# Finishing each token's row in its second expert unit instead of through a plane of partial rows (GLA and MoE block, fp32, one core)

## What is computed

```python
def second_block(...):
    ...
    h2 = rmsnorm_2(x, norm2_g[l])
    x = x + hier_moe(h2, ...)      # 4 groups x 8 experts, D_EXPERT = 256, two experts of one group per token
return rmsnorm_2(x, norm_f_g)

# one expert on its rows:
(jax.nn.silu(xb @ w_gate[e]) * (xb @ w_up[e])) @ w_down[e]
```

```
group 0:  44 50 40 25 15 34 20 12
group 1:  28 14 21 24 21 25 32 29
group 2:  89 43 53 51 35 47 40 14
group 3:   7 30 37 29 11 31 48 25
```

## Time and profile before

| | us |
|---|---|
| median of 3 runs (1300.69 to 1302.65) | 1300.85 |
| the profiled execution, its own time | 1302.32 |
| its span | 1300.0 |
| TensorE busy | 1267.6 (98%) |
| VectorE busy | 613.1 (47%) |
| ScalarE busy | 460.4 (35%) |
| GpSimd busy | 535.5 (41%) |

### The profile page before, as it was taken

The page is one execution under the profiler, slowest core; times in us unless marked ns, Lnnn a source line. Parts: engine busy times, 40 slices in busy tenths (PEclk is TensorE's granted clock), DMA queues, the critical chain, the costliest instruction groups (busy, mean ns, idle before and its releaser), DMA issues.

```text
span 1300.0 us, 18634 instructions
## 1 busy us (share of the span) xinstructions
PE 1267.6 (98%) x6670; PEld 968.7 (75%) x6670; DVE 613.1 (47%) x1162; ACT 460.4 (35%) x770; POOL 535.5 (41%) x685
## 2 busy tenths in 40 slices
PE   8999999999999999999999999999999999999986
PEld 6767777787888888888888788777888875555552
DVE  4868768725542422222225765757243265222225
ACT  5657534435434324133144534145322210000102
POOL 4633323334555655555545664424644211121100
PEclk9999999999999999999999999999999999999999
DMA  7422222112334433434333333312426989999995
GB/s 221 107 65 56 66 58 66 50 49 81 98 96 113 131 97 97 130 98 129 97 98 114 97 93 85 83 49 67 128 81 268 362 323 394 424 421 424 424 423 240
DMA packets 212157, 211.38 MB, mean 163 GB/s; under 512 B 31903, under 2 KB 193425, under 8 KB 200817
## 3 DMA queue, kind: packets, MB, share of 16 engines
q1 hardware_dynamic: 203104, 200.25, 45.8%
q0 software_dynamic: 5184, 8.29, 1.7%
q10 hardware_dynamic: 3796, 1.86, 0.5%
HBM read 205.76 MB, written 16.78 MB: 171 GB/s over the span
## 4 chain that ended last, share of the span: by engine, by line
issue 39%; POOL 31%; PE 26%; DMA 1%; DVE 1%; POOLq 0%; ACT 0%; SPq 0%; DVEq 0%; ACTq 0%
POOL wlo L661 31%; PE bank L2287 8%; PE bank L2304 4%; PE bank L1915 3%; PE bank L1917 3%; PE bank L1916 3%; PE side L1945 2%; DMA y<-y_rows 1%; PE bank L1956 1%; DMA y_rows<-xe,tabi 1%; PE side L1917 1%; PE side L1915 1%; PE side L1916 1%; PE side L2203 1%; PE bank L2419 0%
## 5 line engine op out<-in xcount | busy, mean ns | idle before, releaser
L661 POOL TENSOR_TENSOR wlo<-raw,whi 128x256 fp32r<-128x256 f32 x644 | 498.2, 805 | 524.4 <-ACT whi L785 524.2
L1916 PE MATMUL bank<-actB_lo,whi 128*128 128x512 f32 x608 | 236.7, 389 | 0.0
L1915 PE MATMUL bank<-actB_hi,whi 128*128 128x512 f32 x576 | 227.7, 395 | 0.5 <-POOL wlo L661 0.5
L1917 PE MATMUL bank<-actB_hi,wlo 128*128 128x512 f32 x576 | 224.4, 390 | 0.0
L785 ACT ACTIVATE whi<-raw 128x1024 fp32r<-128x1024 f32 x161 | 169.0, 1051 | 151.8 <-PE bank L1917 124.9
L1915 PE MATMUL bank<-actA_hi,whi 128*128 128x512 f32 x400 | 157.3, 393 | 0.6 <-DVE actA_lo L1201 0.6
L1916 PE MATMUL bank<-actA_lo,whi 128*128 128x512 f32 x400 | 156.1, 390 | 0.0
L1917 PE MATMUL bank<-actA_hi,wlo 128*128 128x512 f32 x400 | 156.1, 390 | 0.0
L2287 PE MATMUL bank<-gu,xeT 128*64 128x256 f32 x1088 | 127.7, 384 | 4.7 <-issue 2.2
L1916 PEld LDWEIGHTS bank<-actB_lo,whi 128*128 128x128 f32 x608 | 114.2, 188 | 24.1 <-issue 1.0
L1915 PEld LDWEIGHTS bank<-actB_hi,whi 128*128 128x128 f32 x576 | 108.1, 188 | 25.9 <-issue 2.3
(11 more groups left out here) (433 smaller groups left out, 1653.0 us busy)
## 6 DMA issues: line engine op xcount, KB each, us to landing
dn<-in_w_exp_down SPq DMA_DIRECT2D x32, 1024.0 KB, 16.0
raw<-in_w_in SPq DMA_DIRECT2D x57, 512.0 KB, 3.8
gu<-in_w_exp_gate SPq DMA_DIRECT2D x28, 1024.0 KB
gu<-in_w_exp_up SPq DMA_DIRECT2D x28, 1024.0 KB
raw<-in_w_up SPq DMA_DIRECT2D x32, 512.0 KB, 3.9
raw<-in_w_down SPq DMA_DIRECT2D x32, 512.0 KB, 3.6
raw<-in_w_out SPq DMA_DIRECT2D x16, 512.0 KB, 3.7
raw<-in_w_in SPq DMA_DIRECT2D x16, 256.0 KB, 3.1
```

Of the source, the lines that this page charges most:

```text
L661: ins = nc.gpsimd.tensor_tensor(wlo[:, slot, at], raw[:, slot, at], whi[:, slot, at].bitcast(F32), ALU.subtract)
L1915: mm(b[:, :], w_hi, hi[:, k, :], start=first, stop=False)
L1916: mm(b[:, :], w_hi, lo[:, k, :], start=False, stop=False)
L1917: ins = mm(b[:, :], w_lo, hi[:, k, :], start=False, stop=last)
```

## The change

The plane of 1,024 partial rows goes. In its place is part_rows, 512 rows of zeros. The unit that has a token first (in unit order) scatters its row there as before; the unit that has it second gathers that row into the token's place in its buffer (a row of it that is first is skipped), adds its own part, norms the whole row and stores it to the output by an indirect DMA. So that both units of a token are not next to each other, experts are now taken one from each group in turn: number n is expert n // 4 of group n % 4. `full` and `late` are worked out in that order. Unit 9's places are now 18 and 17, with number 16 in place 17; units 8 and 9 are "mixed", their tokens' other unit may be any. There are six row buffers instead of five; x is no longer halved. Rows are finished from unit 2 on.

Cut to its core, with the address changes, the overflow loops (not entered) and removed tail parts left out or shortened:

```diff
-GU_BUFS, D_BUFS, X_BUFS = 6, 8, 5
+GU_BUFS, D_BUFS, X_BUFS = 6, 8, 6
...
-    c = (n - 2 * EXTRA_AT + 1) // 2
-    return c - 1 if n % 2 else PAIRS - 1 if n == SPARE else c + PAIRS // 2 - 2
+    return 0 if n == SPARE - 1 else n - SPARE
...
-    return n if n < 2 * EXTRA_AT else None
+    return EPG * (n % NG) + n // NG if n < 2 * EXTRA_AT else None
...
+FINISH_FROM = 2
+MIXED_E = (EXTRA_AT, EXTRA_AT + 1)
...
-                for n in range(2 * q, 2 * q + 2):
-                    sp.dma_start(y2_rows[n * P:(n + 1) * P, :], zeros[:, :]).then_inc(S("y_zeroed"), 16)
+                sp.dma_start(part_rows[q * P:(q + 1) * P, :], zeros[:, :]).then_inc(S("y_zeroed"), 16)
...
-            for j in range(2):
-                sp.wait_ge(S(f"scattered{j}"), 16 * LAST_E // 2)
-            for i in range(NT):
-                sp.dma_start(y2[:, i, :, :], y2_rows.rearrange("(k t p) n -> t p k n", k=2, p=P)[i])\
-                  .then_inc(S(f"block_in{i}"), 16)
-            for i in range(NT):
-                sp.wait_ge(S("final_out"), i + 1)
-                sp.dma_start(out[i * P:(i + 1) * P, :], y2[:, i, 1, :]).then_inc(S("stored"), 16)
-            sp.wait_ge(S("stored"), 16 * NT)
+            sp.wait_ge(S("rows_stored"), 16 * (UNITS_E - FINISH_FROM))
...
+            def gather_parts(n, tokens, done):
+                pool.indirect_dma_start(xe[:, n, :], None, part_rows, bass.IndirectOffsetOnAxis(ap=tokens, axis=0),
+                                        bounds_check=row_bound, oob_is_err=False).then_inc(done, 16)
+
+            def store_rows(n, tokens, done):
+                pool.indirect_dma_start(out, bass.IndirectOffsetOnAxis(ap=tokens, axis=0), xe[:, n, :], None,
+                                        bounds_check=row_bound, oob_is_err=False).then_inc(done, 16)
+
+            def scattered(q):
+                pool.wait_ge(S(f"scattered{q % 2}"), 16 * (q // 2 + 1))
+
+            def parts_of_unit(q):
+                pool.wait_ge(S("xe_used"), 2 * (q + 1))
+                gather_parts(q % X_BUFS, tabi[:, 2, q:q + 1], S(f"parts_in{q % 2}"))
+
+            def store_unit(q):
+                pool.wait_ge(S("rows_finished"), q - FINISH_FROM + 1)
+                store_rows(q % X_BUFS, tabi[:, 2, q:q + 1], S("rows_stored"))
...
             for q in range(LAST_E):
                 if q == EXTRA_AT - 1:
+                    pool.wait_ge(S("slots_ready"), 2)
                     spare_expert()
+                if q:
+                    scattered(q - 1)
+                if FINISH_FROM <= q + 1 < LAST_E and q + 1 not in MIXED_E:
+                    parts_of_unit(q + 1)
                 pool.wait_ge(S("y_made"), q + 1)
                 scatter(q % X_BUFS, tabi[:, 0, q:q + 1], S(f"scattered{q % 2}"))
-                n = q - 1 + X_BUFS
+                n = q + X_FIRST
                 if n < UNITS_E:
-                    if q == 0:
-                        pool.wait_ge(S("over_listed"), 1)
-                    else:
-                        pool.wait_ge(S(f"scattered{(q - 1) % 2}"), 16 * ((q - 1) // 2 + 1))
+                    if q < 2:
+                        pool.wait_ge(S(("over_listed", "over_ready")[q]), 1)
+                    if q - 2 >= FINISH_FROM:
+                        pool.wait_ge(S("rows_stored"), 16 * (q - 1 - FINISH_FROM))
                     gather(n % X_BUFS, tabi[:, 1, n:n + 1], S(f"gathered{n % X_BUFS}"))
+                if q > FINISH_FROM:
+                    store_unit(q - 1)
+                if q + 1 in MIXED_E:
+                    scattered(q)
+                    parts_of_unit(q + 1)
...
             for_overflow(pool, over, overflow)
+            parts_of_unit(LAST_E)
+            store_unit(LAST_E - 1)
+            store_unit(LAST_E)
...
+            def squares_of(q):
+
+                one_ = slice(q % NT, q % NT + 1)
+                nc.scalar.preload_act_table_set("natural_log_exp_and_others")
+                for n in range(2):
+                    act.wait_ge(*((S("y_made"), q + 1) if q < LAST_E else (S("last_y_made"), n + 1)))
+                    chain(a(side[3][:, :], xe[:, q % X_BUFS, n * L:(n + 1) * L], ACT.Square, accum_out=gw[:, 10 + n, one_]))
+                    if n == 0:
+                        chain(a(gw[:, 3, one_], gw[:, 10, one_], ACT.Identity, scale=1.0 / D, bias=eps_t[:, :]))
+                chain(a(gw[:, 14, one_], gw[:, 11, one_], ACT.Ln, scale=1.0 / D, bias=gw[:, 3, one_]))
+                chain(a(gw[:, 13, one_], gw[:, 14, one_], ACT.Exp, scale=-0.5), S("guess_made"))
             for q in range(LAST_E):
...
                 silu_and_turned(q)
...
+                if q > FINISH_FROM:
+                    squares_of(q - 1)
+                    nc.scalar.preload_act_table_set("silu_and_others")
...
+            squares_of(LAST_E - 1)
             for_overflow(act, over, overflow)
+            nc.scalar.preload_act_table_set("silu_and_others")
             silu_and_turned(LAST_E)
...
+            squares_of(LAST_E)
...
+            apart = gw[:, 9, :]
+            chain(v.tensor_scalar(pos_q[:, :], pos[:, :], ROWS - 0.5, None, ALU.is_lt))
+            chain(v.tensor_tensor(rest, two, one, ALU.subtract))
             dve.wait_ge(S("table_full"), 1)
             chain(v.tensor_scalar(tabi[:, 1, 0:EXTRA_AT], bank[1][:, 0:EXTRA_AT], float(SKIP), None, ALU.add), S("rows_ready"))
+            chain(v.tensor_tensor(rest, rest, const("iota")[:, 0:EPG].unsqueeze(1).broadcast_to([P, NT, EPG]), ALU.mult))
+            chain(v.tensor_reduce(apart, rest, AX, ALU.add))
             for n, pick in ((4, one), (5, two)):
                 chain(v.tensor_tensor(rest, pick, logit, ALU.mult))
                 chain(v.tensor_reduce(gw[:, n, :], rest, AX, ALU.add))
             chain(v.tensor_tensor(gw[:, 6, :], gw[:, 5, :], gw[:, 4, :], ALU.subtract), S("shifted"))
-            second_rows = placed[:, NT:2 * NT, 0, 0:LATE]
-            chain(v.scalar_tensor_tensor(second_rows, picks8[:, NT:2 * NT, 0:LATE], float(L), second_rows, ALU.mult, ALU.add))
+            firsts, seconds = slice(0, NT), slice(NT, 2 * NT)
+            for mine, other, after in ((firsts, seconds, ALU.is_lt), (seconds, firsts, ALU.is_gt)):
+                chain(v.scalar_tensor_tensor(vals[:, mine, 0], apart, 0.0, pos_q[:, other], after, ALU.mult))
+            chain(v.scalar_tensor_tensor(vals[:, :, 0], vals[:, :, 0], float(L), row_at[:, :], ALU.mult, ALU.add))
+            chain(v.tensor_tensor(placed[:, :, 0, 0:LATE], picks8[:, :, 0:LATE], every(vals[:, :, 0], LATE), ALU.mult))
...
             def y_of(q):
...
+                if q >= FINISH_FROM:
+                    dve.wait_ge(S(f"parts_in{q % 2}"), 16 * ((q - FINISH_FROM) // 2 + 1))
...
+            def finish(q):
+
+                one_ = slice(q % NT, q % NT + 1)
+                dve.wait_ge(S("guess_made"), guesses[0] + 1)
+                chain(v.tensor_tensor(gw[:, 12, one_], gw[:, 10, one_], gw[:, 11, one_], ALU.add))
+                refine(gw[:, 12, one_], gw[:, 13, one_], D, gw[:, 14, one_], gw[:, 15, one_])
+                if q < LAST_E:
+                    dve.wait_ge(S(f"scattered{q % 2}"), 16 * (q // 2 + 1))
+                chain(v.scalar_tensor_tensor(xe[:, q % X_BUFS, :], xe[:, q % X_BUFS, :], gw[:, 13, one_], gfin[:, :],
+                                             ALU.mult, ALU.mult), S("rows_finished"))
...
             def late_columns():
...
+                chain(v.scalar_tensor_tensor(by_group_of(bend), by_group_of(every_expert), full, group_ids, ALU.is_equal, ALU.mult))
+                chain(v.tensor_reduce(group, bend, AX, ALU.add))
+                chain(v.tensor_scalar(shift, group, float(1 - NG), late, ALU.add, ALU.mult))
+                chain(v.tensor_scalar(by_group_of(bend), group_ids, group, -1.0, ALU.is_equal, ALU.mult))
+                chain(v.scalar_tensor_tensor(in_turn, bend, shift, every_expert, ALU.mult, ALU.add))
+                chain(v.tensor_scalar(last_group, last_group, shift, None, ALU.add))
                 chain(v.tensor_scalar(column_of, every_expert, full, late, ALU.is_gt, ALU.mult))
-                chain(v.tensor_tensor(column_of, every_expert, column_of, ALU.subtract))
-                for at, by in ((LATE + PAIRS // 2, LATE + 1.0), (NE + LATE, -8.0), (LATE, 1001.0 - LATE)):
-                    chain(v.tensor_scalar(bend, every_expert if at == LATE else column_of, at - 0.5, by, ALU.is_ge, ALU.mult))
+                chain(v.scalar_tensor_tensor(column_of, column_of, float(NG), bend, ALU.mult, ALU.mult))
+                chain(v.tensor_tensor(column_of, in_turn, column_of, ALU.add))
+                chain(v.tensor_scalar(column_of, column_of, 1.0 - LATE, None, ALU.add))
+                chain(v.tensor_scalar(bend, column_of, float(ROWS // 2), None, ALU.mult))
+                chain(v.tensor_tensor(cmp_[:, :, :], bend.unsqueeze(2).broadcast_to([P, NE, 7]),
+                                      steps64[:, 0:7].unsqueeze(1).broadcast_to([P, NE, 7]), ALU.is_ge))
```

(26 more changed lines are left out.)

190 lines of the change are left out of this document (94 added, 96 removed).

## The result

The changed kernel takes 1315.9 us (median of 4 runs, 1313.54 to 1317.52), the kernel before, beside it, 1301.75 us (4 runs, 1300.69 to 1305.13). The ratio is 1.0104 with a 95% interval of 1.0084 to 1.0124: slower by about 1%, or 13.5 us by the ratio (the medians lie 14.2 us apart). The forecast was 1307.8 us, 6.9 us slower. The sign held, and so did the range of 1299 to 1317 us, by 1.1 us; the forecast's own range, 1302 to 1312, did not, and the move was twice the forecast.

A forecast was written before the change was run, and what follows sets the result against it. TensorE, the weights and POOL's queue stood close together, with a latency-chain tail behind. Span 1300.0 + 18.8 (net at E, the end of unit 15's y) - 11.9 (tail) = 1306.9; +6.9 on the median gave 1307.8 us, range 1299 to 1317.

The forecast's parts named there:

- the spare place in turns with the weights: POOL's queue before unit 9: expert 31's 3.15 MB alternates packets with the weight queue, taking 14.4 us.
- resumption of unit 9's gates: TensorE's first gates of unit 9, waiting for the spare place, resume at 1180.9, +12.4 us, early +2.8 included.
- the weights' own delay: Weight loads up to E, the end of y(15): 0.8 + 7.4 + 3.8 for further rows = 12.0 us.
- a late parts(9) and a dearer queue: Range's upper side: parts(9) landing later, +5, and POOL's four transfers at 3.2 us each, +6.
- The tail: From E, the end of unit 15's y, to the span's end: 21.0 us instead of 32.9, gaining 11.9.
- a store that I price with the lone gather, 4.4: Last store in the tail, priced at 4.4 us like a gather with no weights on the way; upper end 8.1.
- The given-back term: Unit 15: its 0.45 us wait for weights and 1.7 us of slow matmuls go, -2.2 us.
- The mixed units: Units 8 and 9 wait for parts: +0.4 at hid(9), +6.5 at hid(10), 1.7 for matmuls at 1.2 GHz.
- the early tables: Extra DVE work ahead of and in the first units: +0.8, +0.6 and +1.4, sum +2.8 us.
- Weights bound: Rival, 0.12: spare moves at nearly full rate, mixed units' waits stay covered; 12.0 at E, 1301 us, no change.
- Spare place skipped: Faster rival, 0.12: flag late stays 1, spare transfers move nothing; span 1292.7, or 1299.8 with mixed waits; 1296 us.
- POOL's queue full: Slower rival, 0.12: four transfers at 3.2 us take 12.8 against a 12.09 beat; units 10 to 12 follow, +6, 1314 us.

The follow-up runs named there:

- second profile: Changed kernel run once more, unedited: 1315.54 us, ratio 1.0102 (4 runs); its profiled execution has a span of 1313.8 us.
- first profile: Profiled execution of the changed kernel's first four runs, unedited: 1313.54 us, span 1311.4 us, the shortest of the eight runs.
- first experiment: Changed kernel with the spare place's rows named past the table, so POOL's three transfers move nothing: 1310.12 us, ratio 1.0066.
- last variant: Changed kernel, expert order turned by half, unit 9's parts early, POOL leaving early, no spare transfers, parts(8) ahead of gather 11 and store 6: 1298.68 us, ratio 0.9974.

## Why the prediction had the right sign and half the size

**What it got right.** Up to the end of y(15) every mechanism came where it was put: 33 experts read, the spare place in turns with the weights, resumption of unit 9's gates at +13.6 and, in the second profile, +12.1 (forecast +12.4), no wait for parts in units 2 to 7 and 10 to 16, y(9) waiting, +22.0 and +22.8 at unit 10's end (forecast +21.0), and the weights' own delay of 12.0 us (last weight +12.8 and +11.7; 4.6 against +5.1 without the spare place). That the range held owes something to luck: its upper end was for a late parts(9) and a dearer queue, and the time came near it for other reasons.

**What was mis-sized.** Against the second profile, which stands for the median (span +13.8), the forecast's +6.9 lacks 6.9 us:

- *The tail*, +3.2: 24.2 us instead of 21.0. This is the step that failed first of all, "a store that I price with the lone gather, 4.4" and "0.4 to the end as now". The store landed 2.6 us after its issue, less than priced, but the end came 8.5 us after that issue instead of 4.8, because POOL's drain of 5.46 us, hidden in the kernel before, was no term of the sum. The last y, at E+11.8 instead of E+12.3, gave 0.5 back.
- *The given-back term*, +1.9, a wrong cause. I took the slow matmuls of unit 15's down to follow from the 0.45 us wait for weights, and booked 2.2 us as gone. In the first profile they are gone; in the second, with no wait for weights, the down takes 5.22 us all the same. From unit 11's gates to E are 66.6 us there, 66.95 before: of the 2.2 us, 0.3 came.
- *The mixed units*, +2.1. The wait before hid(9) is 2.0 us in the second profile (0.4 forecast). Behind y(9) TensorE waited 4.4 us, not 6.5, and the slow clock cost more than the 1.7 us for it: of the 10.7 us that units 9 and 10 lost after the gates (forecast 8.6) the two waits are 6.4, and what is left, some 4.3, came with 3.4 us at the 1.2 GHz level at 1197 and 6.8 us from 1214, unit 10's down among them.
- *Resumption*, -0.3.

In the first profile the given-back term was right (2.1 us) and the early tables were dearer: TensorE's 2.58 us wait for place_overflow was followed by a table at the 1.2 GHz level, y(1) is 4.6 us late (second profile 3.1, forecast 2.8).

**The rivals.** *Weights bound*: not the first limit, for E lies 8 to 10.5 us above the weights' floor in the changed kernel. There unit 16's down starts 7.5 and 11 us after the last weight; in the three runs where unit 9's parts come early and the silu is where it was (1308.2, 1298.2 and 1298.7 us) it starts 1.0 to 1.1 us after it. The engines have no time to catch up: their share is full (1.00 to 1.02) in all three stretches of the first profile above. So once y(9)'s wait is out, this rival is the rule: E at +12.0 with the spare place, +5.1 without. By the fit that the Trainium skill gives (DMA: Bandwidth & Descriptors, Anatomy of one DMA), as the prediction's estimate had it, the spare place's transfers would take some 9.2 us; here they landed 4.9 us apart, 14.6 us for three, so beside a full weight queue the trace does not agree. *Spare place skipped*: wrong for this order, and where it was made true the time was 1310, not 1296: the rival's span of 1299.8 us "with the mixed waits kept" was the better half of it (its own terms give 1299.5). The first experiment's profile has 1306.7: 3.2 more in the tail and some 3.7 more at E, +15.4. *POOL's queue full*: no; no unit but 8 and 9 waits for it.

**How the costs combine.** Taking away the spare place gave 5.8 us, unit 9's late parts 7.7, both, with the turned order, the drain moved and the skipped transfers gone, 17.4. The queue's chain (spare place, scatter 7, parts 8, scatter 8, parts 9) and the weights run beside each other; E follows the later. That is why the spare place costs 8 us alone on the old kernel, where it moves the weights' floor, and 5.8 on the new, where the chain stands above the floor. What share the early tables have in the final time was read from the traces alone and not tried on the chip.

## What to carry to other kernels

The end of a program is a join of all engines: before making POOL's transfer the last one, look at what its sequencer does between its last issue and the block's end, for here 5.5 us came out of hiding. When a rearrangement changes the order of data-dependent work, run the reference's data through the new order by hand, as that is where one expert too many came from. And price two late things that run beside each other as the later of the two, with the floor of the bytes beside the chain of waits, not as a sum.

## What the runs showed of the hardware

- POOL's DRAIN took 3.01 us in the kernel before and 5.2 to 5.5 us in the changed kernel and its variants, counted from the end of its last issue when that came later. TensorE's took 3.5 to 4.7 us, hidden in every run.
- Three transfers of 128 rows that were all skipped landed 11.2, 12.4 and 13.7 us after issues that are 1.3 us apart, so some 2.5 us behind each other: beside the weights they still held POOL's queue (first experiment).
- An indirect gather beside a full weight queue took 7.8 us to land with nothing ahead of it in POOL's queue (parts(8) of the last variant); with the weights done, stores and gathers took 2.6 to 3.2 us.
- Around the 11.95 us wait TensorE had the 1.2 GHz level for 13.65 us of the trace's clock record, from 1174.6 to 1188.2, through the gates and into unit 8's down. In seven of the fourteen profiles a stretch of 3.4 us at that level also comes in unit 15, behind waits of 1.5 to 1.6 and 0.7 us that are there in all of them; it costs 1.6 us, of the 4.2 us by which y(7) to y(15) differs between the changed kernel's two profiles.
